# Ten of 24 side-product chunks of a weight stream moved from TensorE to VectorE, and the order of work in the layers changed

## The reference

```
for i in range(DEPTH):                       # first block, DEPTH = 2
    u = rms_norm(h, norm_g[i])
    z = u @ w_in[i]                          # 2048 x 7176: 14 chunks of 512 columns, a tail of 8
    o_a, o_b, o_c = three attention mixers of the columns of z
    mixed = concat([o_a*silu(g_a), o_b*silu(g_b), o_c*silu(g_c)])
    h = h + mixed @ w_o[i]                   # "out"
    h = h + (p[i] @ w_ple[i]) * sigmoid(h @ w_pg[i])      # "gate"
x = rms_norm(h, final_g)
# second block
sh1, sc1, gt1, sh2, sc2, gt2       = split(silu(c) @ w_ada + b_ada, 6)      # used for x
csh1, csc1, cgt1, csh2, csc2, cgt2 = split(silu(c_ctx) @ w_ada + b_ada, 6)  # used for ctx
rq, rk, rv, ... = split_in(modulate(x, norm1_g, sh1, sc1) @ w_in)
crq, crk, crv, ... = split_in(modulate(ctx, norm1_g, csh1, csc1) @ w_in)
# then two scans, an output product, and a product with picked experts
```

## Time and profile before

| | before |
|---|---|
| median of 3 runs | 4055.27 us |
| profiled execution: own time | 4056.81 us |
| profiled execution: span | 4055.2 us |
| TensorE busy | 3824.5 us, 94% |
| VectorE busy | 2238.6 us, 55% |
| ScalarE busy | 1571.7 us, 39% |
| data moved | 799.34 MB, 197 GB/s over the span |
| first layer, second layer | 34.92 to 752.51 us, 752.51 to 1491.10 us |
| kv, mvmk | 1562.4 to 1739.8 us, 1742.4 to 1833.4 us |

### The profile page before, as it was taken

How to read it: one execution, slowest core, us unless ns; L and a number is a source line. 1 busy time by engine, 2 the same in 40 slices (tenths; PEclk the granted TensorE clock), 3 DMA queues, 4 the chain that set the end, 5 groups by cost and what they waited for, 6 DMA issues and landing times.

```text
span 4055.2 us, 50512 instructions
## 1 busy us (share of the span) xinstructions
PE 3824.5 (94%) x21362; PEld 3212.6 (79%) x21362; DVE 2238.6 (55%) x2974; ACT 1571.7 (39%) x1558; POOL 101.1 (2%) x145
## 2 busy tenths in 40 slices
PE   7998989899889977999999989999999999999998
PEld 6676766777667655888888879999999999998886
DVE  3346533334554344226574557967745555657777
ACT  3344434334343343113554343335543333333333
POOL 0000000000000000001000000000000000000000
PEclk9999999999999988999999999999999999999999
DMA  6545566654555651224345644556666666666664
GB/s 252 212 157 198 186 238 236 222 210 152 211 194 207 257 186 47 100 89 160 131 144 212 253 153 176 187 190 221 234 229 223 222 223 222 219 228 247 240 237 176
DMA packets 117960, 799.34 MB, mean 197 GB/s; under 512 B 13136, under 2 KB 13520, under 8 KB 29456
## 3 DMA queue, kind: packets, MB, share of 16 engines
q1 hardware_dynamic: 96704, 692.73, 47.5%
q0 software_dynamic: 18768, 82.96, 5.5%
q10 hardware_dynamic: 2304, 20.97, 1.3%
HBM read 752.57 MB, written 44.04 MB: 196 GB/s over the span
## 4 chain that ended last, share of the span: by engine, by line
PE 55%; DVE 5%; ACT 1%; DMA 1%; issue 1%; DVEq 0%; POOLq 0%; ACTq 0%; POOL 0%; SPq 0%
PE ps L270 17%; PE ps L272 17%; PE ps L271 17%; DVE ring_r L284 1%; PE ps L1602 1%; DMA ring<-in_stream_dram 1%; PE ps L1462 1%; DVE z L2993 0%; DVE act L2757 0%; PE ps L1411 0%; PE ps L1425 0%; DVE z L2989 0%; DVEq L251 0%; DVE z L3047 0%; DVE z L3044 0%
## 5 line engine op out<-in xcount | busy, mean ns | idle before, releaser
L284 DVE TENSOR_TENSOR ring_r<-ring,high 128x2048 fp32r<-128x2048 f32 x384 | 878.8, 2291 | 718.8 <-ACT high L278 715.0
L278 ACT CAST high<-ring 128x2048 fp32r<-128x2048 f32 x384 | 733.9, 1912 | 1263.8 <-DMA ring<-in_stream_dram 1254.9
L2227 DVE TENSOR_TENSOR ring_r<-ring,high 128x2048 fp32r<-128x2048 f32 x176 | 403.1, 2291 | 700.7 <-ACT high L1710 699.3
L270 PE MATMUL ps<-high,z_r 128*128 128x512 f32 x1856 | 734.9, 396 | 15.5 <-DVE ring_r L2227 13.3
L272 PE MATMUL ps<-high,act_r 128*128 128x512 f32 x1888 | 743.0, 394 | 0.0
L271 PE MATMUL ps<-ring_r,z_r 128*128 128x512 f32 x1856 | 728.7, 393 | 0.0
L271 PE MATMUL ps<-act_r,high 128*128 128x256 f32 x2496 | 706.7, 283 | 0.0
L270 PE MATMUL ps<-act_r,high 128*128 128x256 f32 x2304 | 656.5, 285 | 9.7 <-DVE ring_r L284 9.3
L272 PE MATMUL ps<-act_r,ring_r 128*128 128x256 f32 x2304 | 652.5, 283 | 0.0
L270 PE MATMUL ps<-high,h_r 128*128 128x512 f32 x1472 | 600.6, 408 | 52.0 <-DVE ring_r L2227 21.1
L1710 ACT CAST high<-ring 128x2048 fp32r<-128x2048 f32 x176 | 335.3, 1908 | 683.5 <-DMA ring<-in_stream_dram 683.1
(11 more groups left out here) (465 smaller groups left out, 3116.9 us busy)
## 6 DMA issues: line engine op xcount, KB each, us to landing
ring<-in_stream_dram SPq DMA_DIRECT2D x656, 1024.0 KB, 4.8
hidden<-z POOLq DMA_DIRECT2D x32, 512.0 KB, 4.2
gate_matrix<-z ACTq DMA_DIRECT2D x8, 2048.0 KB, 7.2
r<-gate_matrix POOLq DMA_DIRECT2D x32, 512.0 KB, 6.6
z<-hidden POOLq DMA_DIRECT2D x32, 512.0 KB, 7.0
r<-in_w_ple_dram POOLq DMA_DIRECT2D x2, 2048.0 KB, 12.5
merge_gates<-r ACTq DMA_DIRECT2D x8, 512.0 KB, 4.8
r<-merge_gates POOLq DMA_DIRECT2D x4, 1024.0 KB, 5.8
```

The source lines that it names most:

```text
L270: pe.matmul(out, lhs[0], rhs[0], start=start, stop=False)
L278: sc.copy(high[:, j, :], ring[:, j, :]).then_inc(piece_high[j], 1)
L284: dve.tensor_tensor(ring_r[:, j, :], ring[:, j, :], high[:, j, :], ALU.subtract).then_inc(piece_low[j], 1)
L2227: dve.tensor_tensor(ring_r[:, b, :], ring[:, b, :], high[:, b, :], ALU.subtract).then_inc(piece_low[b], 1)
```

## The change

It has seven parts.

- adaLN: 7 chunks a layer stay in the layers, their pieces at single slots (`ADA_SLOTS`). The other ten, for the row of c alone, are computed on VectorE while kv and mvmk's first chunk run: for each piece four operations of 128x512, each a multiply-add with one column of silu(c) (`ada_part`), into a sum in `z`. For each weight chunk two adaLN chunks come through the same ring buffers; the order is written out for SyncE and VectorE. TensorE sums over the partitions by short matmuls with ones (`sum_ada`, 32 in mvmk, 8 in mqrq).
- The first two "in" chunks are interleaved (`IN_PIECES`); TensorE waits for the x tiles of a piece, not for all eight.
- The "out" pieces: order changed, and in slots 60 and 61 both pieces' first halves come first (`parts_of`).
- The rounds of the selection, ropes and one mask on VectorE go to other slots.
- In slots 38 to 53 VectorE does a slot's side work ahead of its difference (`SIDE_FIRST`).
- mvmk and mqrq begin without the barrier of stages (`FLOWING`).
- mod_cols makes one column set later, in mvmk (`keep_early`).

```
+IN_PIECES = [(0, 0), (0, 1), (0, 2), (1, 0), (1, 1), (1, 2), (0, 3), (1, 3)] + [(i, j) for i in range(2, N_IN) for j in range(PIECES)]
-OUT_PIECES = [(0, 0), (1, 0), (0, 3), (1, 3), (0, 1), (0, 2), (1, 1), (1, 2)] + [(c, j) for c in (2, 3) for j in range(PIECES)]
+OUT_PIECES = [(0, 0), (1, 0), (0, 3), (1, 3), (0, 1), (1, 1), (0, 2), (1, 2)] + [(c, j) for c in (2, 3) for j in range(PIECES)]
-ADA_SLOT = (1, 6, 11, 16, 28, 33, 38, 43, 58, 63, 68, 73)
+ADA_SLOTS = ((5, 8, 9, 11), (14, 15, 16, 17), (28, 30, 31, 32), (35, 36, 37, 38), (41, 43, 44, 45), (57, 59, 61, 63), (76, 78, 80, 83))
+        SIDE_FIRST = range(38, 54)
+        FLOWING = ("mvmk", "mqrq", "scan")
...
             # SyncE, kv and mvmk
+            for j in range(3):
+                load_weights(0, j)
+            for m in range(KV_ADA):
+                load_ada(m, 0, 0)
+                load_weights(m, 3)
+                load_ada(m, 1, 0)
+                load_ada(m, 0, 1)
+                load_weights(m + 1, 0)
+                load_ada(m, 1, 1)
+                load_ada(m, 0, 2)
+                load_weights(m + 1, 1)
+                load_ada(m, 1, 2)
+                load_ada(m, 0, 3)
+                load_weights(m + 1, 2)
+                load_ada(m, 1, 3)
...
+                        if q == OUT_SLOT + 4:
+                            return [(q, (0, 1)), (q + 1, (0, 1))]
+                        if q == OUT_SLOT + 5:
+                            return [(q - 1, (2, 3)), (q, (2, 3))]
+                        return [(q, range(PIECE_KT))]
...
             # TensorE, mvmk's first chunk, after its second piece
+                                elif name == "mvmk" and par == 0 and j == 1:
+                                    pe.wait_ge(evac[1], EVAC0[name])
+                                    pe.wait_ge(piece_used[3], ada_used(3, 1))
+                                    sum_ada(0, 8, 7)
...
             # VectorE, layers
-                            if l or q >= 3:
+                            if (l or q >= 3) and q not in SIDE_FIRST:
                                 split(l, q)
                             if l:
                                 side(l - 1, q + SLOTS)
                             side(l, q)
+                            if q in SIDE_FIRST:
+                                split(l, q)
...
             # VectorE, kv and mvmk
+                    def ada_part(m, i, j):
+                        dve.wait_ge(piece_full[j], 16 * ada_used(m, i))
+                        if j:
+                            dve.wait_ge(piece_used[j - 1], ada_used(m, i))
+                        o = ada_sums(2 * m + i)
+                        for q in range(PIECE_KT):
+                            k = PIECE_KT * j + q
+                            w, c = ring[:, j, q * CHUNK:(q + 1) * CHUNK], col(C_SILU + 2 * k)
+                            if k == 0:
+                                a = dve.tensor_scalar(o, w, c, None, ALU.mult)
+                            else:
+                                a = dve.scalar_tensor_tensor(o, w, c, o, ALU.mult, ALU.add)
+                            if q < PIECE_KT - 1:
+                                chain(dve, "dve", a)
+                        a.then_inc(piece_used[j], 1)
+                    def stream_kv(m, evacuate):
+                        ada_part(m, 0, 0)
+                        low(m, 3)
+                        ada_part(m, 1, 0)
+                        ada_part(m, 0, 1)
+                        low(m + 1, 0)
+                        ada_part(m, 1, 1)
+                        ada_part(m, 0, 2)
+                        low(m + 1, 1)
+                        dve.wait_ge(piece_used[3], place(kv_chunk(m), 1, 1))
+                        evacuate()
+                        ada_part(m, 1, 2)
+                        ada_part(m, 0, 3)
+                        low(m + 1, 2)
+                        ada_part(m, 1, 3)
```

More of the change, by code:

```diff
@@ L1320, in _ @@
+                        for q in range(SLOTS):
+                            for p, blocks in parts_of(q):
+                                products(l, p, blocks)
                             if l:
@@ L1351, in _, with sum_ada @@
                 elif name in ("mvmk", "mqrq"):
+                    def sum_ada(first, n_, bank):
+                        for n in range(n_):
+                            for b in range(4):
+                                mm = pe.matmul(ps[:, bank, 4 * n + b:4 * n + b + 1], ada_sums(first + n)[:, b * P:(b + 1) * P], ones[:, 0:1], start=True, stop=True)
+                        mm.then_inc(ada_turned, 1)
                     def turn_gates():
@@ L1979, in out_m @@
                                 sc.copy(raw_c[:, b, :], ps[:, b, 0:TOK]).then_inc(evac[1], 1)
-                    stream_split(sc, split_act, "mvmk", 1, out_m, looped=False)
+                    for m in (4, 5):
+                        split_act(sc, kv_chunk(m), (3,))
+                        split_act(sc, kv_chunk(m + 1), range(3))
+                        sc.wait_ge(piece_used[3], place(kv_chunk(m), 1, 1))
+                        out_m(0, m % 2)
                 elif name == "mqrq":
@@ L2208, in _ @@
                 if after:
-                    split_act(sc, (0, 2 * PAIR0[after], ADA_BEFORE[after]), range(3))
+                    split_act(sc, kv_chunk(0), range(3))
                 end(sc, "act")
@@ L2700, in out_m, with keep_early @@
                                 dve.tensor_copy(raw_c[:, b, :], ps[:, b, 0:TOK]).then_inc(evac[1], 1)
[L2701 removed]
+                    def keep_early():
+                        dve.wait_ge(ada_turned, ADA_L + 1)
+                        c0 = 4 * ADA_L
+                        dve.tensor_tensor(adac[:, c0:c0 + 32, 0], ps[:, 7, 0:32], adac[:, c0:c0 + 32, 1], ALU.add).then_inc(ada_done, 1)
+                        dve.wait_ge(ada_done, ADA_L + 1)
+                        chain(dve, "dve", dve.tensor_scalar(modc[:, 2, :], adac[:, SC2:SC2 + KT, 0], 1.0, None, ALU.add))
+                        dve.tensor_tensor(modc[:, 2, :], modc[:, 2, :], cols[:, C_N2:C_N2 + KT], ALU.mult)
+                        out_m(0, 0)
+                    stream_kv(4, keep_early)
+                    split_dve(dve, kv_chunk(5), (3,))
+                    split_dve(dve, kv_chunk(6), range(3))
+                    dve.wait_ge(piece_used[3], place(kv_chunk(5), 1, 1))
+                    out_m(0, 1)
                 elif name == "mqrq":
@@ L3181, in _ @@
                 if after:
-                    split_dve(dve, (0, 2 * PAIR0[after], ADA_BEFORE[after]), range(3))
+                    split_dve(dve, kv_chunk(0), range(3))
                 end(dve, "dve")
```

201 lines of the change are left out of this document (118 added, 83 removed).

## The result

The changed kernel took 3953.06 us (median of 4 runs, 3945.97 to 3957.74) against 4053.32 us of before, a ratio of 0.9746 with a 95% interval of 0.9722 to 0.9771. It is faster, by 100 us. I had forecast 3905, so 152 less; the direction held and the time lies within the range that I gave (3862 to 3972), but the gain came out a third smaller, and the time is 8 us above the narrower range that went with the forecast (3880 to 3945).

The account below looks back on a forecast made before the run. TensorE, busy 94% of the span, was taken as the bound, its waits being for a place in an order. From 4056.81 us: -50 work, -97 waits, -39 clock, +34 kv = -152, so 3905 us; range 3862 to 3972.

Parts of the forecast that it names:

- half the waits stay: Rival, layers: waits cured one by one, ScalarE or another side step next; waits -54, clock -28, 3959 us; chance 0.15.
- adaLN work off TensorE: Layers: 10 of 24 adaLN chunks leave, each four pieces of 1.04 us and a turn of 0.81; -50 us.
- waits in the layers: Layers: of TensorE's 107.2 us idle, only the L1083 wait and some ring waits stay; -97 us, bounds -54 to -107.
- clock in the layers: Layers: with the long waits gone, most of the loss to a slower granted clock returns; -39 us, between 25 and 51.
- kv stretch: kv and mvmk: VectorE's adaLN sums make the trip 12.3 us against TensorE's 10.95; +34 us, bounds +10 to +50.
- Part (a): Layers: spread adaLN pieces let the ring look three slots ahead, taking most of the 30.5 us at ring_r.
- Part (d): Slots 38 to 53: VectorE's side work ahead of its difference; slot 39's 3.0 us fits into 5.89 us idle.
- Part (b): Slots 60 and 61: first halves first, so L2388's mixed tiles (8.7 us wait, first layer) are needed later and met.
- Part (c): Second layer's start: interleaved first chunks ask for tiles later, curing the 8.2 us wait for L2234.
- 38.9 us from that difference: mvmk: from the first chunk's third-piece difference to the second chunk, VectorE's evacuation and early columns included; 38.9 against TensorE's 21.9.
- kv is hidden: Rival, kv: transfers land earlier than 4.8 us, only the sums' wait and 32 matmuls stay; +10, 3881 us; chance 0.12.
- The two slower ones: Rivals: slower by the order of slots 38 to 53 (chance 0.02); slower by kv, trips of 20.8 us (0.01).

Follow-up runs that it names:

- e3: The changed kernel with VectorE's side work ahead of its difference in slots 36 to 53 instead of 38 to 53; 3936.71 us, ratio 0.9706.
- e4: The changed kernel with ScalarE too doing its side work ahead of its rounding in slots 38 to 53; 3937.74 us, ratio 0.9701.
- e2: The changed kernel with no slots in which VectorE does its side work first; 3961.83 us, ratio 0.9758.
- e8: The changed kernel with the adaLN pieces of six of a layer's seven chunks in four slots in a row; 3946.05 us, ratio 0.9730.
- e10: The changed kernel with the out pieces in the order of before and without the halves; 3961.18 us, ratio 0.9762.
- e12: e11 with ScalarE's copies ahead of the third rounding for mvmk's first chunk only; 3906.18 us, ratio 0.9631 of before.
- e5: The changed kernel with three quarters of VectorE's adaLN sums in kv and mvmk left out; 3929.92 us, ratio 0.9681.
- e1: The changed kernel with the 32 short matmuls of the sums after the last piece of mvmk's first chunk, not its second; 3939.78 us, ratio 0.9713.
- e9: The changed kernel with ScalarE copying a finished mvmk chunk's sums out ahead of rounding the next chunk's third piece; 3942.77 us, ratio 0.9725.
- e11: The changed kernel with the edits of e1, e9, e3 and e4 together; 3909.24 us, ratio 0.9642.
- e7: The changed kernel with the selection's rounds one to a slot (32 to 39), mask at 40, both ropes at 34 again; 3947.89 us, ratio 0.9733.

## Why the prediction was right, and what it mis-sized

The direction held, and each term has the sign it was given. The range held because it was widened by the tail of the rival "half the waits stay" (3959, up to 3975): the narrower range of the forecast, 3880 to 3945, did not reach 3953, and two of its three terms, the waits (85 to 107) and the clock (25 to 51), came out below their bounds. That the time is so close to the rival's 3959 is chance: its waits were cured less than the measured ones (-54 against -74), and its kv term was smaller. Term by term, against the profiled executions:

| term | forecast | measured |
|---|---|---|
| adaLN work off TensorE | -50 | -50, in the fall of busy time (74.5 in the layers) |
| waits in the layers | -97 | -74.3 |
| clock in the layers | -39 | -24.5 (the rest of the 74.5) |
| kv stretch | +34 | +45.5 |
| other stretches | 0 | +4.1 |
| sum | -152 | -99.3 |

- **The work.** The first row is not measured by itself. What is measured is the fall of busy time by 74.5 us, and I divide it by the forecast's own 49.7. The adaLN rows themselves (L346 and L353, L365 and L372 after) are busy 133.5 us for 24 chunks before and 73.8 for 14 after, so 5.6 and 5.3 us a chunk, 53 to 56 for ten (ends of short rows overlap what follows). The forecast had taken one piece and one turn that were cheaper than the mean, and the clock's part may be 3 to 6 us less than the row says.
- **Waits.** The step that failed is "I keep the wait at L1083 and some 3.5 us of ring waits a layer". What was kept is 11.8 us at `ring_r`, 9.6 at L2582, 7.2 at `st` and 3.9 at L2346. It is the rival of the half-cured waits in small, "ScalarE or another side step comes next": e3 and e4 took the two side waits away, each by putting side work ahead of a late piece on one more engine or slot. The waits for side steps at the second layer's start and at slot 60 are gone, as forecast, and so are those at slots 33, 41, 44 and 72, which the forecast had not priced one by one.
- **Slot 39.** Here the mechanism was wrong, not only a size. The prediction says that "a side step that was ready stood behind a piece that was late" and that the 3.0 us of side steps fit into 5.89 us of idle time. They were not ready: ScalarE's exponentials, whose sums they need, ended at 374.11, behind ScalarE's own rounding. VectorE's new order won 1 us there in both layers (e2), the wait only moved one softmax step ahead (3.57 and 3.61 us, where 3.64 and 5.40 had been), and it went when ScalarE did its side work first (e4). A row at `st` over 2 us in TensorE's waits was one of the prediction's own signs against it, and it came.
- **Part (a)** gave the end of ring waits to the spreading of pieces. e8 shows that the spreading does not do it; that the number of pieces does is argued by exclusion. **Part (d)** was the side work ahead of the difference; e2 shows that it is worth 3 us beside the other edits, by the wait at L1170. **Part (b)** is borne out by e10. Part (c), the interleaved first chunks, was not tried alone; the wait at the second layer's start is gone (8.2 us before). Of the 74.3 us of waits that went, the experiments give some 10 to single edits (e2, e10); the rest is the changes together.
- **The bound for slot 49** in (d), at most 1 us of new waiting, held: no wait of 1 us or more stands there. One of 2.84 stands at slot 45.
- **Clock.** Forecast 39 us, measured 24.5, just under the lower bound of 25. In the first 76 us of the first layer, where TensorE hardly idled, the granted clock was 0.86 in the changed kernel's profile and 0.98 in that of e3, whose code there is the same (0.96 in the kernel before, whose code there is another):

```profile
24.00:100.00 76.00, 76.00 (x344) 62.31 (x343) 22.11 (x21) 22.15 (x28) 1.64 (x2) 0.86 0.51 185
```

```profile
24.00:100.00 76.00, 74.47 (x378) 60.02 (x378) 28.40 (x32) 28.00 (x38) 1.63 (x2) 0.98 0.59 224
290.00:360.00 70.00, 65.13 (x328) 50.64 (x327) 45.84 (x124) 32.59 (x61) 0.00 (x0) 0.98 0.55 196
```

  So some 8 to 9 us of this term's shortfall are that one execution's, and the profiled one is the slowest of its four (the median lies 4.7 us lower). The other part is the clock after the waits that stayed, 0.93 in the window from 290 to 360 us, where e3 (first window) shows 0.98 and e12 1.00.
- **kv.** The trip was sized well. The multiply-add of 128x512 with a column took 752 ns at the median (forecast 0.75), four of them 3.11 (3.15); trips are 11.8 to 12.3 for the most part, and 13.3 to 13.5 with copies or a late transfer (forecast 12.3, and 1.4 for the copies). The Trainium skill (VectorE: DVE Perf Modes, the TRN2 errata) gives 691 ns for a tensor_tensor of this size, so this case's trace has 60 ns more for the multiply-add with a column operand. The first ring wait of a microsecond came 113 us into kv, ten pieces in, not six; the third piece of mvmk's first chunk was ready at 1626.00, 211.9 us into kv, and 18 pieces of 10.95 are 197.1: 14.8 late, forecast 15.4. e5 confirms the term: without three quarters of the sums 18.8 us go.
- The step that failed is "38.9 us from that difference": it was 55.4. Of the 16.5 more, 5.6 are the queue of transfers, held behind the third piece by 32 short matmuls at half clock (13.7 us, forecast 7, behind a wait of 5.22), so that VectorE's copies ended at 1670.5 instead of 1664.9; 10.8 are ScalarE's copies, which the prediction left out: it followed SyncE, VectorE and TensorE, and of ScalarE only the roundings. e1 and e9 show the two apart (7.1 and 11.1 us earlier at the second chunk), and e12 has them both: 16.2 us back. The kv term as a whole, +45.5, still lies within its bounds of 24 to 50.
- The Trainium skill (DMA: Bandwidth & Descriptors, Anatomy of one DMA) would make a transfer of 1 MB 4.4 us by its fit, an estimate, and the fit is for transfers issued through GpSimd, while these are issued by SyncE. The transfers of weight pieces in kv and mvmk took 4.8 us at the median (L937, 4.7 to 8.2), so the row of before was the better size. Of two issued within 0.4 us of each other the later one took 6.9 us for the most part (1620.3 and 1607.1, for two), more than the 5.6 of the prediction's upper bound; these were adaLN pieces.
- **The rivals.** That kv is hidden did not come: ring waits of 9.2 us and trips above 10.95. The two slower ones did not: side work first cost no ring wait over 2.84 us in slots 38 to 53, and in kv and mvmk's first chunk no trip passed 14 us, once under way, but the one behind the held queue. Of the signs named for the windows, layers of 630 to 645 us, idle time under 15 us in each and a clock of 0.99 in both were missed (665.6 and 653.3, 16.5 and 16.4, 0.97 and 0.99).

## What to carry to other kernels

Where a wait is cured on one engine by putting ready work ahead of late work, look at the same place on every other engine that handles the late piece: here ScalarE's exponentials and copies stood behind the same transfer as VectorE's steps. When a chain is costed through several engines' orders, write down each engine's next wait, the evacuations too, and ask what stands behind an in-order wait that you add or move; a short piece of TensorE work ahead of a product can hold the queue of transfers. And before a wait is put down to an order, look when the inputs of the step behind it were ready: the exponentials' rows stood in the trace of the kernel before. Undo the parts one by one, too: of the four that were undone in the layers, three (the spread of pieces, the places of the rounds, the order in slots 38 to 53) were worth 3 us or less.

## What was not expected of the hardware

Short matmuls with one moving column ran at a granted clock of 0.50, although they stood back to back for 13.7 us after a wait of 5.22 (0.21 us a record). A wait isn't needed for that: placed behind 22 us of products (e1) they took 9.1 us, the first 5.0 at a clock of 1.00 (46 records, 0.11 us each) and the rest at about half, with TensorE busy all the time; in e5, with nothing waited for, it was 0.50 from 1612.0 on, 2.5 us after their start.

```profile
1637.00:1642.00 5.00, 5.00 (x46) 4.95 (x44) 4.82 (x8) 0.00 (x0) 0.00 (x0) 1.00 0.31 97
1642.00:1647.00 5.00, 4.31 (x22) 4.22 (x22) 1.32 (x2) 1.15 (x1) 0.00 (x0) 0.52 0.93 362
```

And the granted clock of the same, almost fully busy first 76 us of the layers was between 0.83 and 0.98 in twelve executions of the same code there (0.83 in e10 and e11, 0.98 in e3, e7 and e9); the difference of 0.15 is up to 11 us of the whole, and these runs don't show what sets it.
